# Ten Strassen pairs with two plain input tiles ahead, in place of nine pairs with four: the start of a hybrid RG-LRU / Mamba-2 / MoE decoder layer on one core

## The reference

```python
h = rms_norm(x, norm_mix)
proj = h @ w_in                       # 1024 x (5*1024 + 16) columns
lru_x, lru_gate, ssd_z, ssd_xbc, ssd_dt = split(proj)
u   = causal_dwconv(lru_x)            # feeds the RG-LRU
xbc = silu(causal_dwconv(ssd_xbc))    # 4 taps; feeds the SSD chunks
dt  = softplus(ssd_dt + ssd_dt_bias)
...
x = x + concat([y_lru, y_ssd]) @ w_out
x = x + hier_moe(rms_norm(x))
out = rms_norm(x)
```

## Time and profile before

| | before |
|---|---|
| time, median of 3 runs | 1392.35 us (1391.93 to 1393.84) |
| the profiled execution | 1394.85 us |
| its span in the trace | 1393.0 us |
| busy: PE / DVE / ACT / POOL | 1356.7 / 1054.7 / 880.6 / 545.8 us |
| granted TensorE clock, mean of the span | 0.988 |

### The profile page before, as it was taken

The page is one execution under the profiler, slowest core; times in us unless marked ns, Lnnn a source line. Parts: engine busy times, 40 slices in busy tenths (PEclk is TensorE's granted clock), DMA queues, the critical chain, the costliest instruction groups (busy, mean ns, idle before and its releaser), DMA issues.

```text
span 1393.0 us, 20478 instructions
## 1 busy us (share of the span) xinstructions
PE 1356.7 (97%) x6655; PEld 1115.3 (80%) x6655; DVE 1054.7 (76%) x1153; ACT 880.6 (63%) x1088; POOL 545.8 (39%) x496
## 2 busy tenths in 40 slices
PE   8999999999999999799999999999999999999995
PEld 6878888887788878688888788888888888888882
DVE  8962355568877879710577899999999999999987
ACT  5444455386777686200134788788888888888864
POOL 2677888535445456648002122122112122222232
PEclk9999999999999999999999999999999999999998
DMA  5133211433332337415224999999999999999977
GB/s 209 38 106 118 91 46 47 159 100 93 100 94 93 115 93 241 129 46 178 106 121 146 364 391 388 366 355 372 379 376 392 381 387 381 395 385 393 379 271 283
DMA packets 105074, 317.20 MB, mean 228 GB/s; under 512 B 18987, under 2 KB 19899, under 8 KB 104881
## 3 DMA queue, kind: packets, MB, share of 16 engines
q1 hardware_dynamic: 94144, 296.43, 58.3%
q0 software_dynamic: 10864, 19.91, 3.8%
HBM read 295.73 MB, written 39.99 MB: 241 GB/s over the span
## 4 chain that ended last, share of the span: by engine, by line
PE 84%; DVE 8%; ACT 2%; DMA 2%; issue 2%; POOL 1%; SPq 0%; ACTq 0%; DVEq 0%; POOLq 0%
PE ps L1195 38%; PE ps L737 13%; PE ps L841 12%; PE ps L1021 9%; PE ps L1182 2%; DVE XBX L1994 1%; PE ps L1103 1%; PE ps L1215 1%; PE ps L949 1%; PE ps L965 1%; DVE YSL L2006 1%; PE ps L926 1%; PE ps L762 1%; PE ps L933 1%; DVE XBB L1732 1%
## 5 line engine op out<-in xcount | busy, mean ns | idle before, releaser
L2233 DVE TENSOR_TENSOR split_c<-ring_gu,split_c 128x1024 fp32r<-128x1024 f32 x132 | 155.5, 1220 | 0.0
L2395 POOL TENSOR_TENSOR GH<-raw,ones 128x512 fp32r<-128x512 f32 x61 | 80.1, 1313 | 183.1 <-PE ps L737 126.6
L1195 PE MATMUL ps<-split_c,XTH 128*128 128x512 f32 x528 | 141.3, 389 | 0.0
L1604 ACT ACTIVATE split_c<-ring_gu 128x1024 fp32r<-128x1024 f32 x132 | 132.3, 1052 | 1.1 <-PE ps L1195 1.1
L2233 DVE TENSOR_TENSOR split_b<-ring_gu,split_b 128x1024 fp32r<-128x1024 f32 x98 | 116.6, 1218 | 0.0
L1195 PEld LDWEIGHTS ps<-split_c,XTH 128*128 128x128 f32 x528 | 99.1, 188 | 21.0
L1195 PE MATMUL ps<-split_b,XTH 128*128 128x512 f32 x392 | 107.9, 397 | 1.2 <-DVE XTL L2242 1.2
L737 PE MATMUL ps<-XH,GH 128*128 128x512 f32 x336 | 106.9, 399 | 0.5 <-POOL GL L2402 0.5
L2402 POOL TENSOR_TENSOR GL<-raw,GH 128x512 fp32r<-128x512 f32 x66 | 100.0, 1515 | 15.5 <-ACT GH L1559 10.6
L737 PE MATMUL ps<-XL,GH 128*128 128x512 f32 x336 | 103.7, 390 | 0.0
L737 PE MATMUL ps<-XH,GL 128*128 128x512 f32 x336 | 103.6, 390 | 0.0
(11 more groups left out here) (436 smaller groups left out, 3662.0 us busy)
## 6 DMA issues: line engine op xcount, KB each, us to landing
ring_gu<-in_moe SPq DMA_DIRECT2D x264, 512.0 KB, 5.8
ring_dn<-in_moe SPq DMA_DIRECT2D x132, 512.0 KB, 6.8
raw<-in_win SPq DMA_DIRECT2D x70, 256.0 KB, 2.7
T<-acs_d SPq DMA_DIRECT2D x16, 512.0 KB, 4.9
raw<-in_wout SPq DMA_DIRECT2D x32, 256.0 KB, 2.6
T<-in_x SPq DMA_DIRECT2D x8, 512.0 KB, 6.7
X<-in_x SPq DMA_DIRECT2D x8, 512.0 KB, 3.7
x_d<-X SPq DMA_DIRECT2D x8, 512.0 KB, 2.6
```

The lines of the kernel that those rows point to most:

```text
L1195: mm = pe.matmul(ps[:, bank + h, :], x[:, rows], w[slot % HL][:, h * 512:(h + 1) * 512], start=(k == 0 and n == 0), stop=(last and n == 2))
L1604: act.activation(WH[slot % HL], ring[j], ACT.Copy).then_inc(hi_made, 1)
L2233: dve.tensor_tensor(WL[slot % HL], ring[j], WH[slot % HL].bitcast(F32), ALU.subtract).then_inc(lo_made, 1)
L2395: st.link(pool.tensor_tensor(hi, raw[:, r, :], one.to_broadcast([P, GR]), ALU.mult))
```

## The change

Three things, in words:
1. Tiles 2 and 3 of xbc are made as a pair (the fourth one, after the z pairs) and no longer as plain tiles; so ten pairs, and one plain tile (xbc 1, beside tile 0) ahead of the first pair.
2. The instructions around the first pair are ordered anew: corner stored earlier; its high and low parts made before T2's and T4's low parts; PE waits for each of them at the product that uses it; the softplus series is cut into a part before the first pair's sums and a part behind them; the first pair's a12 low part stands ahead of its s2 sum on POOL.
3. In the first chunk step, u tile 0 goes to banks 2 and 3 and z tile 6 to banks 0 and 1 (before 4, 5 and 6, 7), and the wait for the z tile's reading (`z_act`) moves from the middle of `turn_chunk` to behind it.

```diff
-EARLY = (0, 1, 2, 3)
+EARLY = (0, 1)
-X_PAIRS = [(4, 5), (8, 9), (10, 11), (12, 13), (14, 15), (6, 7)]
+X_PAIRS = [(2, 3), (4, 5), (8, 9), (10, 11), (12, 13), (14, 15), (6, 7)]
...
-        GW = [(GH[:, 0, :], GL[:, 0, :]), (GXH[:, :], GXL[:, :]), (GH[:, 1, :], GL[:, 1, :])]
-        GW_SLOT = (0, 2)
+        GW = [(GXH[:, :], GXL[:, :]), (GH[:, 0, :], GL[:, 0, :]), (GH[:, 1, :], GL[:, 1, :])]
+        GW_SLOT = (1, 2)
...
-            for at, (p, n) in ((6, (0, R22)), (7, (0, R12)), (8, (1, R11)), (9, (1, R21))):
-                sp.wait_ge(g_lo, at + 1)
-                pair_load(p, n)
             sp.wait_ge(xl_ready, TT)
             for n, t in enumerate(XF[0][1]):
                 sp.dma_start(corner_d[n], t.bitcast(F32)).then_inc(corner_out, 16)
+            for at, (p, n) in ((2, (1, R11)), (3, (1, R21)), (4, (0, R22)), (5, (0, R12))):
+                sp.wait_ge(g_lo, at + 1)
+                pair_load(p, n)
...
                 if p == 0:
-                    pe.wait_ge(cv_x, X_NTH[2])
-                    pe.wait_ge(f_ready, f_from + 4)
+                    pe.wait_ge(cv_x, X_NTH[1])
+                    pe.wait_ge(f_ready, f_from + 2)
...
+                if p == 0:
+                    pe.wait_ge(f_ready, f_from + 3)
                 pair_product(p, 5, b22, (T2H, T2L), True)
                 pe.wait_ge(p_copy, copy_from + 3 * p + 3)
+                if p == 0:
+                    pe.wait_ge(f_ready, f_from + 4)
                 pair_product(p, 6, b21, (T4H, T4L), False)
...
-                    granule_mms(AT["u", i], 4, (0, 1), True).then_inc(g_used, 1)
+                    granule_mms(AT["u", i], Y_BANK, (0, 1), True).then_inc(g_used, 1)
...
-                    project(("z", Z_FIRST), 6)
+                    project(("z", Z_FIRST), X_BANK)
                     turn_chunk(i)
+                    pe.wait_ge(z_act, Z_FIRST + 1)
...
-                for n in (13, 11, 9, 7, 5, 3):
+                for n in (13, 11, 9):
                     st.link(dve.scalar_tensor_tensor(p, p, 1.0 / n, s2, ALU.add, ALU.mult))
 
             def softplus_tail(v, e, s, s2, p, out):
 
+                for n in (7, 5, 3):
+                    st.link(dve.scalar_tensor_tensor(p, p, 1.0 / n, s2, ALU.add, ALU.mult))
...
+                if p == 0:
+                    weight_lo(p, 2)
+                else:
+                    pool.wait_ge(w_lo, NF * p + 2)
                 weight_sum(p, SQ[:, :], SQ[:, :], r[R11], ALU.subtract, 3)
-                weight_lo(p, 2)
+                if p > 0:
+                    weight_lo(p, 2)
```

More of the change, by code:

```diff
@@ L268, in build @@
         XF = [[(x_part(XH, k, h), x_part(XL, k, h)) for h in range(2)] for k in range(2)]
-        GW = [(GH[:, 0, :], GL[:, 0, :]), (GXH[:, :], GXL[:, :]), (GH[:, 1, :], GL[:, 1, :])]
-        GW_SLOT = (0, 2)
-        W_RING = [RAWX[:, 0, :], RAWX[:, 1, :]] + [raw[:, n, :] for n in (2, 3, 0, 1)]
+        GW = [(GXH[:, :], GXL[:, :]), (GH[:, 0, :], GL[:, 0, :]), (GH[:, 1, :], GL[:, 1, :])]
+        GW_SLOT = (1, 2)
+        W_RING = [RAWX[:, 0, :], RAWX[:, 1, :]] + [raw[:, n, :] for n in range(RAW)]
         w_raw = lambda p, n: W_RING[(4 * p + n) % len(W_RING)]
@@ L433, in build @@
         X_BANK, Y_BANK = 0, 2
-        u_bank = lambda i: Y_BANK if i else 4
         first_next = AT["u", 0] + 2
-        CONV_BANK = {0: 5, 1: 2, 2: 0, 3: 6}
+        CONV_BANK = {0: 5, 1: 0}
         for p, (j1, j2) in enumerate(PAIRS):
@@ L527, in pair_loads @@
                     pair_load(p, R21)
-                sp.wait_ge(w_lo, NF * (p - 1) + F_NAMES.index("a12") + 1)
+                sp.wait_ge(w_lo, NF * (p - 1) + F_NAMES.index("a12" if p > 1 else "s3") + 1)
                 pair_load(p, R22)
@@ L557, in _ @@
             pair_loads(NP - 1)
[L558 to L561, removed]
+            sp.wait_ge(w_lo, NF * (NP - 1))
+            for n in range(2):
+                granule(FIRST_LATE + n)
             sp.wait_ge(w_mm, NF * (NP - 1) + F_NAMES.index("s3") + 1)
@@ L855, in pair_project @@
                 b11, b12, b21, b22 = pair_banks(p)
-                if p == 0:
-                    pe.wait_ge(cv_x, X_NTH[1])
-                elif p == 1:
+                if p == 1:
                     pe.wait_ge(sp_arg, 1)
                     pe.wait_ge(cv_x, X_NTH[0])
-                else:
+                elif p >= 2:
                     pair_read(p - 2, 0)
@@ L1381, in _ @@
             form_hi(T2H, F22, 2)
+            weight_hi(0, 0)
             silu_tile(0)
[L1383 to L1391, removed]
             weight_hi(0, 1)
@@ L1395, in _ @@
             weight_hi(0, 2)
-            conv_first(3)
+            conv_first(1)
+            form_hi(T4H, F21, 3)
             pair_copy(0, 0)
@@ L1400, in _ @@
             weight_hi(0, 4)
+            silu_tile(1)
+            act.wait_ge(sp_arg, 1)
+            link(act, act.activation(sv["e"], sv["nab"], ACT.Exp), sp_exp, 1)
             weight_hi(0, 5)
@@ L1514, in lru_tap @@
                 wait(act, hr_out, 16 * (i - 1))
-                act.activation(HRR[i % 2], pair(u_bank(i)), ACT.Identity,
+                act.activation(HRR[i % 2], pair(Y_BANK), ACT.Identity,
                                bias=param("lru_cb", i), scale=param("lru_cw", 24 + i)
@@ L1521, in _ @@
                     lru_tap(i)
-                    z_tile(Z_FIRST, 6, 0)
+                    z_tile(Z_FIRST, X_BANK, 0)
                 turned_b(i)
@@ L1812, in _ @@
             link(dve, dve.tensor_tensor(F21, F21, F22, ALU.subtract), f_sum, f_from + 3)
+            form_lo(XF[0][1][1], F12, XF[0][1][0], 3)
+            conv_tile(1)
             form_lo(T2L, F22, T2H, 2)
-            conv_tile(1)
-            form_lo(T4L, F21, T4H, 3)
+            form_lo(T4L, F21, T4H, 4)
             dve.wait_ge(vt_mm, 1)
@@ L1836, in _ @@
             st.link(dve.tensor_copy(colv[:, 1, :, :], th(dt)))
-            pair_sums(0)
             dve.wait_ge(acs_mm, 1)
@@ L1954, in lru_taps @@
                 dve.wait_ge(tap_u, i + 1)
-                conv_taps(HRR[i % 2], u_bank(i), lambda k: param("lru_cw", KT * k + i), u_ready,
+                conv_taps(HRR[i % 2], Y_BANK, lambda k: param("lru_cw", KT * k + i), u_ready,
                           i + 1)
```

17 lines of the change are left out of this document (3 added, 14 removed).

## The result

The changed kernel took 1395.91 us (median of 19 executions, 1392.71 to 1398.18), the kernel before on the same chip 1391.93 us (19 executions, 1389.19 to 1394.84). The ratio is 1.0022 with a 95% interval of 1.0013 to 1.0031: 3.1 us slower, 1.8 to 4.3 (the medians alone are 4.0 us apart, the means 3.3). I had forecast +1.0 us and 1393.4 us. The time lies inside the range, near its upper end, but outside the range of the main case (up to 1394.9). The changed kernel is slower, since the interval lies above 1; whether by more than the forecast's measure of 2.8 us, the interval leaves open.

The account below looks back on a forecast made before the run. PE was taken to bound the kernel, so shifts at the start carry to the end. -4.76 us taken away plus waits of 0.7, 2.0 and 3.1 gave +1.0 us, 1393.4 us; range for 8 in 10: 1390.3 to 1396.3.

Parts of the forecast that it names:

- the main case: The sum as worked out, +1.0 us, with its own range of -0.5 to +2.5 us (1391.9 to 1394.9); chance 0.60.
- the forecast's measure of 2.8 us: The smallest change, about 0.2%, that a measurement of this kernel was said to tell from none.
- What the change takes away: 12 matmuls fewer (-2.72), two PE waits for POOL's low parts (-0.63, -1.01), one ahead of four transposes (-0.40); together -4.76 us.
- DVE's large operations meet POOL's: The two take turns: POOL ends 0.9 to 1.15 us behind the DVE operation it meets; DVE pays 0.7 to 1.0.
- Product 2: First pair: PE waits for the first product's copy, queued on ACT behind T4's high part; +0.7 us.
- Product 3: First pair: PE waits for the bank that tile 1's taps on DVE read; +2.0 us.
- Product 5: First pair: PE waits for s2's low part, behind ACT's exponential, whose argument stands behind T2's and T4's low parts; +3.1 us.
- The second pair, taken as nothing: POOL's a12 low part and the copy for product 2 were forecast just in time, 84.8 and 85.1 against 85.3; 0 us.
- The rival in which this pair starves: Second pair: seven POOL operations at 1.62 us make a12's low part late, +1.8; sum +2.8, 1395.2 us; chance 0.20.
- Sum: -4.76 + 0.7 + 2.0 + 3.1 = +1.0 us, 1393.4 us for the median.
- The start does not set the end: Rival: a later stage that waits for a transfer absorbs the start's shift either way; 1392.4 us; chance 0.05.
- elsewhere: Theory of the experiments, not the prediction: the some 2 us missing from the trace come from something slower outside the first pair.

Follow-up runs that it names:

- pool_extra: The changed kernel with one more, unused POOL operation (128x512) behind s4's low part in the first pair; 1395.19 us in one execution.
- exp_late: The changed kernel with the exponential on ACT moved behind the high parts of s2 and a22 and the first pair's third copy; 1396.21 us, ratio 1.0020.
- series_after: exp_late with the whole softplus series behind the first pair's sums on DVE; 1391.82 us, ratio 0.9991 to the kernel before.
- t4_split: t4_late_series with the first of T4's two DVE operations put back ahead of the corner's low part; 1391.88 us, ratio 0.9984 to the kernel before.
- again2: The changed kernel unaltered, run once more on another chip; 1395.59 us, ratio 1.0014 to the kernel before.
- t4_late_series: series_after with T4's two DVE operations behind the corner's low part and tile 1's taps, its ACT high part behind s2's; 1393.73 us, ratio 1.0001.
- lo3_early: t4_split with s3's low part two operations earlier on POOL and the exponential's argument ahead of T4's second operation on DVE; 1392.26 us, ratio 0.9990.
- warm12: The changed kernel with 12 unused matmuls of ones (128x128) on PE ahead of the first pair's product 5; 1394.49 us, ratio 1.0009.
- warm_gap: The changed kernel with 24 unused matmuls of ones (128x128) on PE ahead of the first pair's product 5; 1395.50 us, ratio 1.0018.
- again: The changed kernel unaltered, run once more; 1395.98 us, ratio 1.0016 to the kernel before on the same chip.

## Why the forecast was right in its mechanism and short in its size

The sums below take a matmul at 0.2268 us, as the forecast did.

- **What the change takes away** (-2.72, -0.63, -1.01, -0.40): as put. The two waits for POOL's low part are gone, and the four transposes begin at 275.81, 0.87 us behind the eight at 274.94.
- **DVE's large operations meet POOL's**: as put, in place and nearly in size (3.27, 3.27 and 3.42 us for a forecast of 3.0 to 3.3; T4's first operation took 2.69 for 3.1), and pool_extra shows cause and effect.
- **Product 2, +0.7**: PE was ready at 55.27 + 24 x 0.2268 = 60.71 and began at 61.05, 0.34; restarting costs 0.15 more (the twelfth matmul ends its turn at 63.92, not 63.77). 0.5 us.
- **Product 3, +2.0**: 65.83 - 63.92 = 1.9 and 0.1 for the restart. 2.0 us. The profile names POOL's low part and not the taps; DVE's taps end at 65.63 and that low part at 65.69, so the two end together, and I had named only one.
- **Product 5, +3.1**: 74.34 - 71.38 = 2.96 and 0.1. 3.0 us at full clock. The exponential was made at 71.87 to 72.19, forecast 72.5, and the first pair ended at 79.86, forecast 79.8. exp_late shows that it was the exponential that held this product.
- **The second pair, taken as nothing**: its own waits are 0.2 us ahead of product 2, and 0.3 over the pace in the 8.48 us of the 36 matmuls behind it. The copy that had 0.2 us in hand was just late, and a12's low part was not. The rival in which this pair starves did not come about: of POOL's operations from its first sum to a12's low part, one took the 1.62 us that the rival gave to seven. exp_late shows how near it lay, for once product 5 doesn't wait, the same copy is 3.4 us late.
- **Sum**: the three waits are 5.5 us for a forecast of 5.8, the second pair 0.5 for 0, and some restarts behind the waits of before went with them (its 27.50 us for 120 matmuls hold 0.28 us of it). All pairs are 1.3 us longer, forecast 1.4 (the +1.0 without the transposes' 0.40).
- **The start does not set the end**: refuted. 580 us on, the second block of the output projection's first pass follows the first input sum by 596.97 us after and by 597.73 before, with a first block of 45.12 against 46.65; take that out and +0.8 is still there. The times of series_after and t4_split, changed at 50 to 90 us alone, say the same.

**The term that was sized too small** is that of product 5, "+3.1 us": it costs PE's wait by its length alone. Behind a wait of that length PE's granted clock is sometimes at the 1.2 GHz level, and it was in again2 (+1.3 us), exp_late and pool_extra (+2.5 us), and behind 2.53 us in t4_split; it was not in the changed kernel's three other traces, nor behind any wait of 2.13 us or less in series_after, t4_late_series and lo3_early. In the kernel before no wait of this stretch is over 0.9 us, so the cost is one that the change brings in.

How much of the missing size that is stays open. Over the four comparisons of the changed kernel with the one before, the means differ by 3.3, 2.6, 2.2 and 2.1 us, on average 2.6, of which 0.8 is structure: 1.8 us to explain. One trace in four with 1.3 us would give 0.3, half of the executions with 1.3 to 2.5 some 0.6 to 1.3. Filling the wait brought 1.0 us (warm12) and paid for 2.06 us of delay (warm_gap).

Two more readings bound it. First, *elsewhere* has no share in the schedule: matched matmul by matmul, the changed kernel's four traces keep their distance from before's within 0.1 us over 280 to 560, 605 to 740 and 800 to 1350 us, and move only where the granted clock differs. Second, every execution reports its mean clock. Over 55 executions of the changed kernel it is 0.98876, over the 99 of before that have one on record 0.98912; within either kernel 0.001 less goes with some 1.1 us more, so this difference is worth 0.4 us, and at the same reported clock the changed kernel is still 1.9 us longer, where the traces' structure has 0.8. The mean clock is a rough measure, because it doesn't say where the low stretch fell: both again and the changed kernel's first trace have 0.81 over 10 to 28 us, yet the first input sum begins at 30.9 us in one and at 29.0 in the other. And the filled kernels' clock (0.9900, 0.9904) lies above before's too, so the fill may gain more than the wait had cost. About 1 us is thus in neither the traces' structure nor the reported clock, and its cause is open.

That the time lies within the stated range at all is in part luck: the main case ended at 1394.9, and the range reached 1396.3 for the sake of a rival, the starving second pair, that did not come about.

## What to carry to other kernels

Moving a helper engine's small operations in among another engine's large ones can cost both of them: lay the two timelines side by side and see who begins second, since here a POOL operation that did ended some 1.2 us behind the DVE operation (up to 2.1 us longer than alone), and the DVE operation that followed took 0.4 to 1.1 us longer. Then ask which of the operations held up PE waits for; reordering moved the meetings and did not remove them, and yet the versions differed by 2 us. When a wait is removed, look for the next one on the same path before claiming its length: behind product 5's 3.0 us lay the series' 3.4 us. Only versions with both moves were faster than the changed kernel (series_after by 4.2 us, t4_split by 3.7, each on one chip), while exp_late, with one, was not. And on a kernel that PE bounds, cost a wait like these of 2.5 to 3.6 us by its length and a further 1 to 2.5 us as a risk, which a single good trace does not show (here four of seven traces with such an unfilled wait had it); compare several.

## What the runs showed that I had not expected

- The instants of the schedule repeat to a few hundredths of a microsecond over executions and chips (waits of 1.74 to 1.76 and 2.77 to 2.81 us), while the total time moves by 2.5 us to either side: what varies between the traces is the granted clock of four stretches, and the start, where the first input sum begins at 28.8 to 31.0 us; most plainly a first block of 192 matmuls that takes 45.1 to 46.7 us where the next one takes 43.70.
- Equal waits are followed by unequal clocks: 2.80 us by 1.00, 2.81 us by 0.66.
- A matmul of 128x128 with f32 operands leaves two records and takes 0.22 us (48 records, 5.3 us for 24), nearly as much as one of 128x512 in the kernel's own products (0.227 us).
- A POOL operation that begins 0.01 us behind DVE's waits for all of it and takes 3.42 us; one that begins 0.02 us ahead takes 1.30 us, and DVE's takes 3.42.
